# Where VectorE scales the attention rows, and in which order TensorE forms the cross-attention queries

## The reference, cut to what matters

```python
xn = rmsnorm(h, norm_mix);  q, k, v, u = split(xn @ w_in)
y_a = dilated_attention(q, k, v, rel_bias)            # 8 heads of 64, three dilation patterns
y_b = s5_mixer(u, ...)                                # linear recurrence over time, then a gate
h = h + concat(rmsnorm(y_a) * g_out_attn, rmsnorm(y_b) * g_out_ssm) @ w_out
hn = rmsnorm(h, norm_xattn)
q = hn @ w_xq                                         # 4 heads of 128
s = q @ k_mem.T * 128 ** -0.5;  p = softmax(s)        # 256 memory tokens
h = h + (p @ v_mem) @ w_xo
h = h + moe(rmsnorm(h, norm_moe))                     # top 4 of 32 experts, clamped SwiGLU
return rmsnorm(h, norm_final)
```

## Time and profile before

| | |
|---|---|
| median of three runs | 2458.14 us |
| the profiled execution's own time | 2458.14 us |
| its span in the trace | 2456.5 us |
| PE busy | 2413.8 us, 98% of the span |
| PEld busy | 1952.9 us, 80% |
| DVE busy | 709.5 us, 29% |
| ACT busy | 382.2 us, 16% |
| POOL busy | 505.6 us, 21% |
| mean granted TensorE clock | 0.992 of full |

### The profile page before, as it was taken

One profiled execution on the slowest core, in us unless ns is written; L12 is line 12 of the kernel. 1 busy time (PEld: TensorE's weight loads), 2 busy tenths in 40 slices (PEclk: granted clock), 3 DMA queues, 4 the chain that ended last, 5 costly groups with the idle time before them and its releaser, 6 DMA issues.

```text
span 2456.5 us, 35421 instructions
## 1 busy us (share of the span) xinstructions
PE 2413.8 (98%) x14592; PEld 1952.9 (80%) x14592; DVE 709.5 (29%) x1859; ACT 382.2 (16%) x846; POOL 505.6 (21%) x989
## 2 busy tenths in 40 slices
PE   8999999999997999999999999999999999999997
PEld 5455566445566899999999999999978788787875
DVE  3122287223553221222222222222222222222223
ACT  2020176112331000000000010001100010000002
POOL 4988881320011000000010000001000000000001
PEclk9999999999997999999999999999999999999999
DMA  8450110500026356556667777878998888988886
GB/s 230 109 99 35 69 53 33 176 34 35 17 113 272 141 186 213 178 208 227 234 236 241 256 264 253 281 267 290 320 341 325 319 331 312 350 320 318 318 311 263
DMA packets 242001, 526.77 MB, mean 214 GB/s; under 512 B 32029, under 2 KB 45597, under 8 KB 241836
## 3 DMA queue, kind: packets, MB, share of 16 engines
q1 hardware_dynamic: 226736, 482.44, 53.4%
q0 software_dynamic: 13968, 41.85, 7.7%
q10 hardware_dynamic: 1132, 0.16, 0.0%
HBM read 489.91 MB, written 48.24 MB: 219 GB/s over the span
## 4 chain that ended last, share of the span: by engine, by line
PE 96%; DVE 2%; issue 1%; DMA 1%; ACT 1%; POOL 0%; POOLq 0%; SPq 0%; ACTq 0%; DVEq 0%
PE ps L2068 44%; PE ps L2099 12%; PE ps L1290 11%; PE ps L635 10%; PE ps L2078 8%; PE ps L2048 2%; PE ps L937 1%; PE ps L925 1%; PE ps L949 1%; PE ps L2056 1%; PE ps L617 1%; PE ps L1297 1%; PE ps L717 1%; PE ps L2089 1%; PE ps L622 1%
## 5 line engine op out<-in xcount | busy, mean ns | idle before, releaser
L2068 PE MATMUL ps<-xT,wch 128*128 128x128 f32 (+16 forms) x8192 | 1087.0, 294 | 1.0 <-issue 1.0
L2068 PEld LDWEIGHTS ps<-xT,wch 128*128 128x128 f32 x8192 | 1068.4, 191 | 16.2 <-issue 7.2
L2155 DVE TENSOR_SCALAR glu<-ps,b1s 128x128 f32<-128x128 f32 (+16 forms) x256 | 96.2, 376 | 757.8 <-PE ps L2068 752.7
L2099 PE MATMUL ps<-act,wch 128*128 128x256 f32 (+15 forms) x2048 | 308.7, 313 | 0.0
L2099 PEld LDWEIGHTS ps<-act,wch 128*128 128x128 f32 x2048 | 303.2, 190 | 3.6
L2271 ACT ACTIVATE sg<-glu 128x256 f32<-128x256 f32 (+16 forms) x128 | 58.6, 458 | 1215.4 <-DVE glu L2155 1194.2
L1991 POOL COPY b1s<-b1T 128x16 f32 x32 | 6.2, 195 | 1023.8 <-DVE outT L2173 691.1
L2078 PE MATMUL ps<-wch,act 128*128 128x512 f32 x480 | 208.5, 592 | 0.0
L2078 PEld LDWEIGHTS ps<-wch,act 128*128 128x128 f32 x480 | 90.1, 190 | 107.6 <-issue 107.6
L2000 POOL DMA_INDIRECT acc_dram<-orow,idx_s x47 | 74.8, 1592 | 455.6 <-ACT orow L2255 224.5
L635 PE MATMUL ps<-xnT,wa 128*128 128x512 f32 x384 | 165.6, 592 | 0.0
(11 more groups left out here) (333 smaller groups left out, 2022.9 us busy)
## 6 DMA issues: line engine op xcount, KB each, us to landing
wch<-in_w SPq DMA_DIRECT2D x128, 2048.0 KB, 12.1
wch<-in_w SPq DMA_DIRECT2D x128, 1024.0 KB, 8.6
b2bc<-in_b SPq DMA_DIRECT2D x16, 512.0 KB
wa<-in_w_in SPq DMA_DIRECT2D x3, 2048.0 KB, 10.7
acc_dram<-h SPq DMA_DIRECT2D x10, 512.0 KB, 2.8
skew_dram<-line_dram SPq DMA_DIRECT2D x8, 576.0 KB, 12.0
xrow<-in_x SPq DMA_DIRECT2D x8, 512.0 KB, 8.3
wa<-in_w_xkv SPq DMA_DIRECT2D x2, 2048.0 KB, 7.8
```

Source lines behind the costliest of these rows:

```text
L2068: last = nc.tensor.matmul(m.ps[:, 2 + g % 3, part * WIN:part * WIN + W], m.wch[2 * h + part][:, k, cols], m.xT[i % 2][:, k, 0:W], start=(k ...
L2099: last = nc.tensor.matmul(m.ps[:, 5 + j % 3, 0:W], m.wch[4 + k // 2][:, k % 2, j * P:(j + 1) * P], m.act[i % 2][:, k, 0:W], start=(k == 0) ...
L2155: v.tensor_scalar(m.glu[:, b, n, 0:W], bank[:, 0:W], m.b1s[:, i % 2, j:j + 1], LIMIT, ALU.add, ALU.min).then_inc(glu_ok, 1)
```

## The change

There are two edits.

1. `finish` for pair p is called at the end of turn 8p + 14: turns 14, 22 and 30 for pairs 0, 1 and 2, where they stood at 22, 24 and 30. Its waits are the same, and so is the last pair's.
2. The query products go head by head, (0, 0), (0, 1), (1, 0), (1, 1) first, and TensorE waits once, ahead of the first, for the last two copies of half 1, where each product waited for those of its own half. `emit_scores` looks for its product at the place that follows.

```diff
-        finished_at = {2 * NB + 6: 0, 2 * NB + 8: 1, 3 * NB + 6: 2}
...
                 raise_rows(i - 3)
-            if i in finished_at:
+            if i >= 7 and (i - 7) % NB == NB - 1:
                 for half in range(2):
-                    finish(dve, finished_at[i], half)
+                    finish(dve, (i - 7) // NB, half)
...
-    def xq_tile(i):
-
-        return divmod(i, 2) if i >= 4 else (i % 2, i // 2)
-
...
-            c, half = xq_tile(i)
+            c, half = divmod(i, 2)
...
                 transposes([(m.xn, m.xnb)[half][:, n, k * P:(k + 1) * P] for n in range(4)])
+        copied(pe, at["HT"] + 14)
+        copied(pe, at["HT"] + 15)
         pe.wait_ge(wxq_in, 16)
 
-        def queries(lo, hi):
-            for i in range(lo, hi):
-                c, half = xq_tile(i)
-                for n in (8 * half + 6, 8 * half + 7):
-                    copied(pe, at["HT"] + n)
+        def queries(c):
+            for half in range(2):
                 product(lambda k: m.wd0[:, k, c * P:(c + 1) * P], lambda k: m.hT[:, k, half * 512:(half + 1) * 512], 512, KC)
 
         def emit_scores(blk):
             hd, half = blocks[blk]
-            copied(pe, xq([xq_tile(i) for i in range(8)].index((hd, half))))
+            copied(pe, xq(2 * hd + half))
...
-        queries(0, 4)
+        queries(0)
+        queries(1)
         emit_scores(0)
         emit_scores(1)
-        queries(4, 8)
+        queries(2)
+        queries(3)
```

## The result

The changed kernel takes 2470.59 us, the median of five runs (2469.72 to 2471.83), against 2458.3 for the kernel before in the same comparison. That is 12.3 us more; the ratio is 1.0051, with a 95% interval of 1.0037 to 1.0066. Forecast were 2472.3 us, 14.2 more. The profiled execution of the kernel after has a span of 2469.2 us, 12.7 longer than that of before.

The account below looks back on a forecast made before the run. TensorE, busy for 98% of the span, was taken to bound the kernel. Stall 10.4, low clock 2.5 and queries 1.3 us gave 14.2 on 2458.1: 2472.3 us, 0.6% slower, range 2467.3 to 2478.

Parts of the forecast that it names:

- The wait of VectorE and its releaser: At turn 14, from 349.5 us, VectorE's gain multiplication waits about 11 us for GpSimd's squares, which begin at 359.3.
- TensorE's pause: In the attention, TensorE idles 10.4 us, from 352.9 to 363.4, before the second score unit of step 16.
- The clock: After TensorE's attention pause, 5 us of work run at the low clock, losing 2.5 us; bounds 0, 1.9 and 4.4.
- The queries: Ahead of the first query product, near 574 us, TensorE idles 1.3 us for VectorE's last copy.
- From there the two traces stay parallel to the end: From the queries on, the distance between the traces of before and after was to stay the same.
- a sign of being wrong: The forecast would be wrong if the distance between the two traces shrank in the experts.
- What was counted as nothing: In the attention's other turns, moved gain multiplications and GpSimd's later squares were to cost 0 us.
- stall without the clock: Attention pause costs 10.4 us, but the clock holds or its low stretch is hidden: 2469.8 us; 12 in 100.
- fall again at the queries: Rival: a second clock fall near 575 us adds 1.9 to 4.4 us, about 2475.5 us; 8 in 100.
- The squares were not there in time: Rival: GpSimd's squares precede VectorE's turn 14, so moving the multiplications is free: 2459.4 us; 4 in 100.
- stay low through the attention: Rival: transposes don't count for the clock, so it stays low until the output product: 2535 us; 3 in 100.
- The rule against the rows: At kernel start, transposes shortening from 424 through 350 to 275 ns (5-7, 11-13, 15-17 us) showed transposes raise the clock.

Follow-up runs that it names:

- edit 1 alone: Kernel before with only the gain multiplications moved (turns 14, 22, 30), queries as before: 2469.5 us against 2458.51, ratio 1.0044.
- the busy pause: Kernel with only the gain multiplications moved, plus 84 identity transposes on TensorE ahead of the wait where it pauses: 2468.48 us against 2457.85 before.
- edit 2 by itself: Kernel before with only the queries head by head behind one wait, gain multiplications as before: 2458.74 us against 2458.51, ratio 1.0000.
- the wait alone: Kernel before with the one wait added ahead of the first query product, order of queries unchanged: 2457.81 us against 2457.85, ratio 1.0001.
- turn 18: Kernel with only the gain multiplications moved, but pair 0's at turn 18 instead of 14: 2458.13 us against 2457.85 before, ratio 1.0001.
- squares in the scan: Kernel with only the gain multiplications moved, GpSimd squaring pair 0 between scan steps 115 and 116: 2458.49 us against 2458.51 before, ratio 1.0000.

## Why the prediction was right

The direction, the range and the mechanism held; the sum was 1.5 us too large between the two traces and 1.9 against the medians. Step by step:

- **The wait of VectorE and its releaser.** Right. One wait in front of line 979, ended by the first square, forecast about 11 us, measured 10.2 and, with edit 1 alone, 10.8. The scan's undisturbed pace was taken as 1.59 us; with VectorE waiting its last steps start 1.58 to 1.60 us apart.
- **TensorE's pause, 10.4 us forecast.** 361.75 less 352.2, when the unit could have started, is 9.6 in the profiled execution of the kernel after. 9.4 of it is idle, and with edit 1 alone 10.1. The term was sized from where the scan stood in one execution. In the execution after, the whole attention was 0.8 us early, and the end of the scan 0.8 us further still: the squares began at 357.8, not 359.3.
- **The clock, 2.5 us forecast.** It fell, and cost 1.7 us by the busy pause and 2.1 by half of the 4.1 us of work at the low level: inside the bounds of 1.9 to 4.4 or just below, and below the value taken, since it came back after 4 us and not 5. Between the traces of before and after it is 2.0: the second unit of step 16 starts 8.9 us later, the output product 10.8 (435.77 against 424.93).
- **The queries, 1.3 us forecast.** The pause is 1.38 us. It was taken to last to the end. Between the traces of before and after it does: the queries start 12.2 us later, the first expert matmul 12.5, and the end comes 12.7 later, so "From there the two traces stay parallel to the end" holds for this pair. But in both the clock is low for the same 30.7 us around the start of the experts, and that is luck. With edit 1 alone the distance to before shrinks there from 12.9 to 11.6 us, which the forecast had named as a sign of being wrong. The forecast put nothing down for this stretch, whose length varies by 7 us from run to run. Of edit 2 by itself the medians show hardly anything: alone it comes out 0.2 us over before, and the wait alone level with it.
- **What was counted as nothing** was nothing: the moved multiplications (turn 18, squares in the scan) change no time.
- **The rivals.** By the time alone "stall without the clock" would have won: its 2469.8 is 0.8 us from the median, the forecast 1.7. The trace rules it out, since the clock did fall; the two came so close because the stall was sized too long. The clock did not fall again at the queries. The squares were not there in time, VectorE waited 10.2 us for them. And the clock did not stay low through the attention.
- **The rule against the rows.** The Trainium skill ("TensorE: Matmul & The Clock Gate", Part 4: PE-mode transpose) says that the full clock does not engage for transposes, since they don't count as busy in the same way. The runs here disagree with it for float32 transposes: 84 of them alone held the clock at 1.00. The prediction went the right way, but it misread: 424 to 275 ns is a ratio of 1.5, not of 2. Neighbouring transposes overlap, so their durations are not their pace. The starts carry the argument: in the trace of before the transposes of line 617 start 0.21 us apart until 12.0 us and 0.11 apart from 12.2 on, a ratio of 2, and ahead of that TensorE had done nothing but transposes. Other matmuls (line 646) come from 12.81 to 14.8 us, so the last of the three windows is not one that only transposes led up to.

The forecast's 14.2 less the 12.7 between the two traces is 1.5 us. The start of the attention, 0.8 us earlier in this execution, the pause with 0.8 and the clock with 0.5 make it too large by 2.1, and 0.1 more at the queries and 0.5 behind them go the other way; what makes the 0.5 was not followed up.

## What to carry to other kernels

Before a wait is moved earlier on an engine, look up when its releaser will come, on the releaser's own queue: here two instructions stood behind 128 steps of a serial scan, and the wait was as long as the distance to its end. If the earlier place is wanted, move the released work too; the squares inside the scan made the same place free. A pause of the engine that bounds the kernel can be paid twice, as idle time and as slow work behind it: here one of 9.4 us was, those of 2.0 and 1.4 us in their traces were not. And before two kernels are told apart by 1 or 2 us, look whether the clock took the same course in both.

## What the runs showed of the hardware

- From the last steps of the routing into the start of the experts the granted clock is at its lower level for 23.9, 27.3 or 30.7 us in the thirteen traces of this study, and from the first expert matmul to the end the kernel takes 1678.3 to 1678.8 us with the first length (four traces) and 1679.7 to 1680.9 with the other two. So two executions of one kernel can differ by 2 us through this alone.
- A gain multiplication on VectorE (0.44 us alone) that starts beside a GpSimd operation on two tensors ends 0.3 us behind it: 1.57 us for two, beside the second square, in every kernel that waited.
